# Feed-forward norms: VectorE adds the squares of tiles 1 to 3 only, TensorE sums the rest

## The chip, the cores and the metric

The kernel runs on one core of a Trainium2 chip. The metric is the device time of one execution in microseconds (us), as the median of several runs.

## The reference, cut to what matters

Two transformer blocks run one after the other on 256 tokens of 1024 channels in fp32. The first has neighbourhood attention and a routed mixture of experts and ends with a norm. The second has four layers; in each, attention of one of three kinds and a feed-forward part follow each other, each behind a norm:

```
def rms_norm_2(x, gain):
    var = jnp.mean(xf * xf, axis=-1, keepdims=True)
    return (xf * lax.rsqrt(var + EPS)).astype(x.dtype) * gain
...
    for i in range(DEPTH_2):
        h = modulate(rms_norm_2(x, norm_gain[i, 0]), sh1, sc1)
        ...
        x = x + g1 * y
        h = modulate(rms_norm_2(x, norm_gain[i, 1]), sh2, sc2)
        x = x + g2 * swiglu(h, ffn_w_gate[i], ffn_w_up[i], ffn_w_down[i])
```

The change touches the sum of squares of the second norm of each layer, the one in front of `swiglu`.

## The kernel before, in words

The residual stream `xT` stands transposed: 8 tiles (`KT`) of 128 channels by 256 tokens. A norm needs, for each token, the sum of squares over all 8 tiles and their 128 partitions. ScalarE squares tile by tile into `xsq` (line 1237, semaphore `sq_ready`). VectorE adds tiles 1 to 6 onto tile 0 of `xsq` (`add_squares`, line 1706, semaphore `sq_added`). TensorE multiplies a matrix of ones with tile 0 (line 525) and with tile 7 (line 527), which sums over partitions and leaves the result in every partition of a bank (`norm_of_sums`, semaphore `ssq_done`). ScalarE then takes a logarithm (1241) and an exponential (1243) into `rinv`; VectorE scales `xT` (1669), ScalarE adds the shift and rounds (1250), and VectorE makes the low part in `hT` (1680). Norms are numbered by `e`: 5, 7, 9 and 11 are the feed-forward norms of layers 0 to 3, and 6, 8 and 10 the first norms of layers 1 to 3.

All large products are made of three matmuls on a high and a low part (`split_product`, line 559). ScalarE casts a weight tile to its high part (1221, in `split`), and VectorE subtracts to get the low part (1962 for the output projection, 2179 for the first two gate tiles, 2199 and 2201 for the later ones). Each engine runs its own program in order; only semaphores tie them.

Around a feed-forward norm the orders are these. TensorE: the 8 tiles of the output projection, for layers 0 to 2 the first third of the next layer's modulation products (`group_rows`, 32 matmuls of line 617), `norm_of_sums`, for layers 0 to 2 the other two thirds (64 of line 617), and then the first two gate tiles, which take `hT` tile by tile. VectorE: for each output tile `update` (1696, adds the projection to `xT`); behind tile 5 `first_low(0)` and the adds of squares 1 to 3; behind tile 6 `first_low(1)` and the adds of squares 4 to 6; then `take_mods` (three small steps, 1806 to 1813), the update of tile 7, the split of gate tile 2 (2201), and the scaling. ScalarE: the squares of tiles 0 to 5, a cast, the squares of 6 and 7, the cast of gate tile 2, and then the logarithm. GpSimd's queue loads the modulation weights and waits for the matmuls of line 617 to free a buffer; SyncE's queue loads all other weights into a ring of three slots.

Of the kernel before, what the change touches and what calls it, by code (L numbers as in the profile page):

```python
# [14 lines left out]
KT = D // P  # L15
T = 256
# [63 lines left out]
def build(nc, ins, out):  # L80
# [3 lines left out]
    with ctx:  # L84
        offset = {}

        def sb(name, shape):
            offset[name] = -(-nc.sbuf_base // 32) * 32
            return ctx.enter_context(nc.sbuf_tensor(name, shape, F32))
# [5 lines left out]
        def sem(name):  # L95
            return ctx.enter_context(nc.semaphore(name))
# [7 lines left out]
        xsq = sb("xsq", [P, KT, T])  # L104
# [29 lines left out]
        def cst(name, lo=0, n=None):  # L134
            a, b = CONST[name]
            return const[:, a + lo:(a + lo + n) if n else b]

        def vc(name, lo=0, n=None):
            a, b = VEC[name]
            return vec[:, a + lo:(a + lo + n) if n else b]  # L140
# [21 lines left out]
        def split_views(ring, xsq, xn, hT, mixT, work, qk, qn, qr, vv):  # L162
# [56 lines left out]
        sq_added = sem("sq_added")  # L219
# [8 lines left out]
        sq_ready, ssq_done, ln_ms, rinv_ready, xn_ready, h_ready = (  # L228
            sem(n) for n in ("sq_ready", "ssq_done", "ln_ms", "rinv_ready", "xn_ready", "h_ready"))
# [115 lines left out]
        def group_of(i, part):  # L345

            return (0, 0, 1, 3)[part] if i == 0 else 4 * i + part
# [27 lines left out]
        def tiles_before(e):  # L375

            return KT * (e - (e > 3))

        def norm_bank(e):

            return bank[4 if e == 2 or e > 4 and e % 2 else 3]
# [128 lines left out]
        def _(pe):  # L510
            mm = nc.tensor.matmul
# [9 lines left out]
            def norm_of_sums(e):  # L521

                b = norm_bank(e)
                pe.wait_ge(sq_added, (KT - 2) * (e - 4))
                mm(b[:, 0:T], cst("ones"), xsq[:, 0, :], start=True, stop=False)
                pe.wait_ge(sq_ready, tiles_before(e) + KT)
                mm(b[:, 0:T], cst("ones"), xsq[:, KT - 1, :], start=False, stop=True).then_inc(ssq_done, 1)

            def norm_twice():

# [55 lines left out]
            def mix_out(d, k0, k1):  # L586

                n = FIRST["out_0"] + d // 4
                if d % 4 == 0 and k0 == 0:
                    wait_chunk(pe, n)  # L590
                b, at = MIX_TILES[d]
                for k in MIX_ORDER[k0:k1]:
                    m = mm(bank[b][:, at:at + T], chunk3(n, 512)[:, k, d % 4 * P:(d % 4 + 1) * P], mixT[:, k, :],  # L593
                           start=k == MIX_ORDER[0] and at == 0, stop=k == MIX_ORDER[-1], skip_group_check=True)
                return m
# [29 lines left out]
            def ada_columns(dst, row, c):  # L625

                out4 = dst.rearrange("p (h f c) -> p f h c", h=2, f=2)
                for f in range(2):
                    m = mm(out4[:, f], row[:, f * P:(f + 1) * P], cst("sel").rearrange("p (h c) -> p h c", h=2)[:, :, 0:c], start=True, stop=True)
                return m  # L630
# [17 lines left out]
            for n in range(N_HEAD):  # L648
                pe.wait_ge(rows_ready, n + 1)
                m = ada_columns(bank[2][:, 8 * n:8 * n + 8], ada_rows[:, n, :], 2)  # L650
            m.then_inc(ada_cols, 1)

            n = FIRST["mix"]
# [18 lines left out]
            for c in range(2):  # L672
                for t in range(TT):
                    m = mm(bank[4 + c][:, :], f3[:, t, c * P:(c + 1) * P], cst("dft", t * 2 * T, 2 * T), start=t == 0, stop=t == TT - 1)
            m.then_inc(dft_pe, 1)
            pe.wait_ge(dft_act, 2)
            for c in range(2):
                mm(bank[6 + c][:, 0:T], cst("cd"), soft[:, c, 0:T], start=True, stop=False)
                m = mm(bank[6 + c][:, 0:T], cst("sd"), soft[:, c, T:2 * T], start=False, stop=True)
# [3 lines left out]
            for f in range(2):  # L683
                for k in range(2):
                    m = mm(bank[4 + f][:, 0:T], wf[:, k, f * P:(f + 1) * P], prob[:, k, 0:T], start=k == 0, stop=k == 1)
# [68 lines left out]
            for d in range(6):  # L754
                m = mix_out(d, KT - 1, KT)
# [8 lines left out]
            for k in range(KT):  # L764
                pe.wait_ge(h_ready, KT * 2 + k + 1)
                for t in range(TT):
                    m = mm(bank[0][:, t * (G + E):(t + 1) * (G + E)], hT[:, k, t * P:(t + 1) * P], wr[:, k, :],
                           start=(k, t) == (0, 0), stop=k == KT - 1, skip_group_check=True)
            m.then_inc(route_done, 1)

            for t in range(TT):
                for k in range(KT):
                    m = nc.tensor.transpose(bank[4 + 2 * t + k // 4][:, k % 4 * P:(k % 4 + 1) * P], hT[:, k, t * P:(t + 1) * P], cst("ident"))
# [7 lines left out]
               start=False, stop=False, skip_group_check=True)  # L781
# [118 lines left out]
            def rest():  # L900
# [3 lines left out]
                for i in layers:  # L904
# [4 lines left out]
                    if i > 0:  # L909
                        norm_of_sums(4 + 2 * i)  # L910
                        group_rows(group_of(i, 2), "attn", 1)
# [737 lines left out]
        def _(dve):  # L1649
# [39 lines left out]
            def update(c, f, n, a, g):  # L1689

                if f < 3:
                    dve.wait_ge(y_done, MIX_DONE + 6 * (a - 1) + 3 * c + f + 1)
                else:
                    wait_used(dve, n)
                d = 4 * c + f
                V.scalar_tensor_tensor(xT[:, d, :], bank[(4 + d) % 8][:, 0:T], mod[:, g * KT + d:g * KT + d + 1], xT[:, d, :],
                                       ALU.mult, ALU.add).then_inc(x_done, 1)


            def add_squares(e, k0, k1):  # L1700

                for k in range(k0, k1):
                    dve.wait_ge(sq_ready, tiles_before(e) + k + 1)
                    if k > 1:
                        dve.wait_ge(sq_added, (KT - 2) * (e - 5) + k - 1)
                    V.tensor_tensor(xsq[:, 0, :], xsq[:, 0, :], xsq[:, k, :], ALU.add).then_inc(sq_added, 1)

            def normalise_in(e, src):
# [23 lines left out]
            n = FIRST["mix"] + 1  # L1732
# [68 lines left out]
            def take_mods(g):  # L1801

                chunks = chunks_of(g)
                i, lo, n = chunks[0] // 12, 4 * (chunks[0] % 12), 4 * len(chunks)
                dve.wait_ge(halves_landed, 64 * (g + 1))
                V.tensor_tensor(mod[:, lo:lo + n], halves[:, 0, 0:n], halves[:, 1, 0:n], ALU.add).then_inc(halves_sum, 1)
                dve.wait_ge(halves_sum, g + 1)
                V.tensor_tensor(mod[:, lo:lo + n], mod[:, lo:lo + n], vc("b_ada2", MODS * i + lo, n), ALU.add).then_inc(mods_taken, 1)
                dve.wait_ge(mods_taken, g + 1)
                if g == 0 or chunks[0] % 6 == 3:  # L1810
                    half = (chunks[-1] - 3) // 6 % 2
                    at = 3 * KT * half + KT
                    V.scalar_tensor_tensor(gain[:, 2 * half, :], mod[:, at:at + KT], 1.0, vc("gains2", (2 * i + half) * KT, KT),
                                           ALU.add, ALU.mult).then_inc(mods_ready, 1)
# [131 lines left out]
            for k in range(KT):  # L1946
                m = V.scalar_tensor_tensor(xT[:, k, :], xT[:, k, :], vc("normf", k, 1), rinv[:, :], ALU.mult, ALU.mult)
            then(m, "mods")

            for i in layers:  # L1950
# [7 lines left out]
                def low_out(c, f):  # L1958

                    n = FIRST[f"out_{i + 1}"] + c  # L1960
                    dve.wait_ge(attn_hi, out_splits(i) + 4 * c + f + 1)
                    V.tensor_tensor(part["w_gu"](n, f), full["w_gu"](n, f), w_out_hi[f][:, :, :].bitcast(F32),
                                    ALU.subtract).then_inc(attn_lo, 1)
# [211 lines left out]
                def first_low(f):  # L2175

                    dve.wait_ge(w_hi, 4 * split_count(i, 0) + f + 1)
                    n = FIRST[f"gu_{i}"]
                    V.tensor_tensor(part["w_gu"](n, f), full["w_gu"](n, f), w_out_hi[f].bitcast(F32), ALU.subtract).then_inc(w_lo, 1)

                for c in range(2):
                    for f in range(4):
                        if (c, f) == (1, 3):
                            take_mods(group_of(i, 3))
                        update(c, f, FIRST[f"out_{i + 1}"] + c, 1 + i, 2)
                        if c == 0:
                            low_out(1, f)
                        if (c, f) == (1, 1):
                            first_low(0)
                            add_squares(5 + 2 * i, 1, 4)  # L2190
                        if (c, f) == (1, 2):
                            first_low(1)
                            add_squares(5 + 2 * i, 4, KT - 1)
                def split(step, r, f, down=False):

                    dve.wait_ge(w_hi, 4 * split_count(i, step, down) + f + 1 + 4 * RING * r)
                    n = FIRST[f"down_{i}" if down else f"gu_{i}"] + step
                    if down:
                        m = V.tensor_tensor(part["w_down"](n, f), full["w_down"](n, f), part["whd"][f].bitcast(F32), ALU.subtract)  # L2199
                    else:  # L2200
                        m = V.tensor_tensor(part["w_gu"](n, f), full["w_gu"](n, f), part["whi"][f].bitcast(F32), ALU.subtract)  # L2201
                    m.then_inc(w_lo, 1)
# [199 lines left out]
```

## Time and profile before

| what | value |
|---|---|
| median of 3 runs | 2072.74 us (2072.51 to 2072.77) |
| the profiled execution's own time | 2074.49 us |
| its span from the first to the last instruction | 2072.7 us |
| mean granted TensorE clock | 0.974 |
| TensorE busy | 1886.8 us, 91% of the span |
| VectorE busy | 866.9 us, 42% |
| ScalarE busy | 721.5 us, 35% |
| adds of squares on VectorE (line 1706) | 42, 425 ns each |
| records of ones-matmuls (lines 525 and 527) | 14 and 14, two for each matmul |

Times are counted from the span's start. The four feed-forward norms lie at about 851, 1217, 1532 and 1868 us. A matmul's record is longer than the distance to the next one, because matmuls overlap; the chain of waits shows the distances.

### The profile page before, as it was taken

The numbers are of one execution on the slowest core, as the hardware profiler recorded it, in microseconds if no ns is written. First come the engines' busy times: TensorE is split into PE (matmuls) and PEld (weight loads), VectorE is DVE, ScalarE is ACT, GpSimd is POOL, SyncE is SP. The second block draws the span as 40 slices with busy tenths as digits, with TensorE's granted clock in tenths as the row PEclk, the third lists the DMA queues.
The fourth block names the chain that finished last, engine by engine and source line by source line (L and its number), as shares of the span: only waits on it lengthen the run. The fifth ranks groups of instructions, "written<-read, shape, count | busy, mean of one in ns | idle before, by whom it ended". The sixth has DMA issues, their size and how long they took to land.

```text
span 2072.7 us, 39160 instructions
## 1 busy us (share of the span) xinstructions
PE 1886.8 (91%) x16878; PEld 1605.2 (77%) x16878; DVE 866.9 (42%) x1512; ACT 721.5 (35%) x1237; POOL 72.8 (4%) x131
## 2 busy tenths in 40 slices
PE   6999976776677799999999999999999999999998
PEld 4788643444344588999987799998689998989998
DVE  0233311101010454654544565454864556555454
ACT  2111200000000355543432354353553444654443
POOL 0200000000000000100000010000010000000000
PEclk8999999899998999999999999999999999999999
DMA  9457899999999966753762485476284467324433
GB/s 397 190 223 297 328 426 427 428 427 428 427 428 427 422 241 240 300 199 140 287 267 99 164 324 186 155 290 274 93 339 180 177 267 311 130 112 163 172 144 133
DMA packets 42480, 552.48 MB, mean 267 GB/s; under 512 B 6528, under 2 KB 6912, under 8 KB 7040
## 3 DMA queue, kind: packets, MB, share of 16 engines
q1 hardware_dynamic: 33696, 454.17, 55.3%
q0 software_dynamic: 8672, 96.67, 11.3%
q8 instruction: 87, 1.43, 0.3%
q14 instruction: 25, 0.20, 0.0%
HBM read 549.58 MB, written 1.05 MB: 266 GB/s over the span
## 4 chain that ended last, share of the span: by engine, by line
PE 72%; DMA 21%; DVE 4%; ACT 2%; issue 1%; SPq 0%; DVEq 0%; ACTq 0%
PE bank L559 48%; DMA ada_ring<-in_moe_side 15%; PE bank L544 5%; PE bank L617 4%; DMA ring<-in_moe 3%; PE bank L553 2%; PE bank L824 2%; PE bank L593 1%; DMA ring<-in_v 1%; DMA ada_ring<-in_ada_last 1%; PE bank L1067 1%; PE bank L965 1%; PE bank L978 1%; ACT work L1478 1%; PE bank L602 1%
## 5 line engine op out<-in xcount | busy, mean ns | idle before, releaser
L559 PE MATMUL bank<-xsq_parts,ring_parts 128*128 128x256 f32 x1664 | 471.2, 283 | 0.0
L559 PEld LDWEIGHTS bank<-xsq_parts,ring_parts 128*128 128x128 f32 x1664 | 319.5, 192 | 0.0
L559 PE MATMUL bank<-xsq_parts,mixT_parts 128*128 128x256 f32 x704 | 199.2, 283 | 0.0
L559 PE MATMUL bank<-hT_parts,mixT_parts 128*128 128x256 f32 x704 | 199.2, 283 | 0.0
L1221 ACT CAST mixT_parts<-ring 128x1024 fp32r<-128x1024 f32 (+1 forms) x152 | 147.6, 999 | 112.5 <-PE bank L559 100.4
L559 PE MATMUL bank<-xsq_parts,xn_parts 128*128 128x256 f32 x640 | 181.1, 283 | 0.0
L559 PE MATMUL bank<-hT_parts,xn_parts 128*128 128x256 f32 x640 | 181.1, 283 | 0.0
L1895 DVE TENSOR_TENSOR mixT<-mixT,bank 128x128 f32<-128x128 f32 x32 | 9.2, 287 | 339.1 <-ACT mixT L1362 339.1
L559 PEld LDWEIGHTS bank<-xsq_parts,mixT_parts 128*128 128x128 f32 x704 | 135.2, 192 | 0.0
L559 PEld LDWEIGHTS bank<-hT_parts,mixT_parts 128*128 128x128 f32 x704 | 135.2, 192 | 0.0
L1221 ACT CAST xn_parts<-ring 128x1024 fp32r<-128x1024 f32 x96 | 100.0, 1050 | 96.3 <-PE bank L559 94.8
L559 PE MATMUL bank<-work_parts,mixT_parts 128*128 128x256 f32 x448 | 127.0, 284 | 0.0
L2201 DVE TENSOR_TENSOR ring_parts<-ring,xn_parts 128x1024 fp32r<-128x1024 f32 x80 | 97.7, 1225 | 68.4 <-ACT xn_parts L1221 65.7
L559 PEld LDWEIGHTS bank<-xsq_parts,xn_parts 128*128 128x128 f32 x640 | 122.9, 192 | 0.0
L559 PEld LDWEIGHTS bank<-hT_parts,xn_parts 128*128 128x128 f32 x640 | 122.9, 192 | 0.0
L824 PE MATMUL bank<-ada_ring,xsq 128*32 128x256 f32 x1024 | 76.8, 451 | 46.5 <-DMA ada_ring<-in_moe_side 46.5
L544 PE MATMUL bank<-hT,ring 128*128 128x256 f32 x512 | 116.1, 383 | 2.4 <-DMA ring<-in_na 1.7
L2199 DVE TENSOR_TENSOR ring_parts<-ring,mixT_parts 128x896 fp32r<-128x896 f32 x64 | 69.5, 1091 | 99.9 <-ACT mixT_parts L1221 99.9
L544 PEld LDWEIGHTS bank<-hT,ring 128*128 128x128 f32 x512 | 95.7, 190 | 19.2 <-issue 3.0
L2201 DVE TENSOR_TENSOR ring_parts<-ring,mixT_parts 128x1024 fp32r<-128x1024 f32 x88 | 104.2, 1222 | 13.7 <-ACT mixT_parts L1221 10.9
L824 PE MATMUL bank<-ring,xsq 128*32 128x256 f32 x1024 | 64.7, 396 | 44.3 <-DMA ring<-in_moe 43.5
L824 PEld LDWEIGHTS bank<-ada_ring,xsq 128*32 128x32 f32 x1024 | 34.5, 125 | 86.6 <-DMA ada_ring<-in_moe_side 62.5
(356 smaller groups left out, 4048.4 us busy)
## 6 DMA issues: line engine op xcount, KB each, us to landing
ring<-in_moe SPq DMA_DIRECT2D x48, 2048.0 KB, 27.2
ada_ring<-in_moe_side SPq DMA_DIRECT2D x48, 2048.0 KB, 26.0
ada_ring<-in_ada POOLq DMA_DIRECT2D x45, 2048.0 KB, 13.1
ring<-in_gu SPq DMA_DIRECT2D x44, 2048.0 KB, 7.7
ring<-in_down SPq DMA_DIRECT2D x32, 1408.0 KB, 6.3
ring<-in_na SPq DMA_DIRECT2D x12, 2048.0 KB, 10.3
ring<-in_out SPq DMA_DIRECT2D x10, 2048.0 KB, 8.2
ring<-in_qk SPq DMA_DIRECT2D x8, 2048.0 KB, 9.5
```

The costliest lines, as they stand in the source:

```text
L544: m = mm(dst, w[:, k, lo:lo + P], h[:, k, :], start=k == 0, stop=k == KT - 1)
L553: m = mm(dst[:, t, :], h[:, k, t * P:(t + 1) * P], w[:, k, lo:lo + n], start=k == 0, stop=k == KT - 1)
L559: m = mm(dst, w[a], x[b], start=start and (a, b) == (0, 0), stop=stop and a == 1, skip_group_check=shared)
L593: m = mm(bank[b][:, at:at + T], chunk3(n, 512)[:, k, d % 4 * P:(d % 4 + 1) * P], mixT[:, k, :], start=k == MIX_ORDER[0] and at == 0, stop= ...
L602: m = mm(o[64 * h:64 * h + 64, a:b], vv[:, kt, 64 * h:64 * h + 64], probT[:, h, c:d], start=i == 0, stop=i == len(tiles) - 1, skip_group_c ...
L617: m = mm(dst[32 * q:32 * q + 32, :], c[:, kk, :], w[:, kk, q % 2 * T:(q % 2 + 1) * T], start=k == 0, stop=k == 3)
L824: m = mm(bank[0][CAP * q:CAP * (q + 1), 0:T], xg[:, 4 * c + k, h * CAP:(h + 1) * CAP], w[:, k, q * T:(q + 1) * T], start=(c, k) == (0, 0), ...
L965: mm(bank[6 + h][:, 0:T], cst("suffix"), sp_[:, 0:T], start=True, stop=False, skip_group_check=True)
L978: m = mm(bank[4 + h][:, a:b], qk[hp, keys], qk[hp, tokens], start=True, stop=True)
L1221: return nc.scalar.copy(o, i)
L2199: m = V.tensor_tensor(part["w_down"](n, f), full["w_down"](n, f), part["whd"][f].bitcast(F32), ALU.subtract)
L2201: m = V.tensor_tensor(part["w_gu"](n, f), full["w_gu"](n, f), part["whi"][f].bitcast(F32), ALU.subtract)
```

## The change

For the feed-forward norms VectorE adds squares 1 to 3 only; the call for squares 4 to 6 is gone. TensorE multiplies ones with the summed tile 0 and then with tiles 4, 5, 6 and 7, one after the other, with a wait for each square. The layers' first norms keep six adds and two matmuls. As norms now differ in their number of adds, a helper counts the adds before a norm, and waits on `sq_added` use it.

```diff
@@
+        def adds_before(e):
+
+            return sum(3 if n % 2 else KT - 2 for n in range(5, e))
+
@@
             def norm_of_sums(e):
 
                 b = norm_bank(e)
-                pe.wait_ge(sq_added, (KT - 2) * (e - 4))
+                pe.wait_ge(sq_added, adds_before(e + 1))
                 mm(b[:, 0:T], cst("ones"), xsq[:, 0, :], start=True, stop=False)
-                pe.wait_ge(sq_ready, tiles_before(e) + KT)
-                mm(b[:, 0:T], cst("ones"), xsq[:, KT - 1, :], start=False, stop=True).then_inc(ssq_done, 1)
+                for k in range(1 + adds_before(e + 1) - adds_before(e), KT):
+                    pe.wait_ge(sq_ready, tiles_before(e) + k + 1)
+                    m = mm(b[:, 0:T], cst("ones"), xsq[:, k, :], start=False, stop=k == KT - 1)
+                m.then_inc(ssq_done, 1)
@@
                     if k > 1:
-                        dve.wait_ge(sq_added, (KT - 2) * (e - 5) + k - 1)
+                        dve.wait_ge(sq_added, adds_before(e) + k - 1)
@@
                         if (c, f) == (1, 2):
                             first_low(1)
-                            add_squares(5 + 2 * i, 4, KT - 1)
```

## Rows read from the trace of the kernel before

**Rows 1.** The page: shares of the chain that ended last, by engine.

```profile
PE 72%; DMA 21%; DVE 4%; ACT 2%; issue 1%; SPq 0%; DVEq 0%; ACTq 0%
```

**Rows 2.** Chain of waits, layer 0's norm: start us, us, what.

```profile
849.33 1.86 PE bank L617 x32
851.20 0.63 PE bank L525 x2
851.83 0.43 PE bank L527 x2
852.26 3.59 PE bank L617 x64
855.85 14.27 PE bank L559 x118
```

**Rows 3.** Timeline of VectorE, layer 0: start us, us, instruction [idle before].

```profile
853.25 1.28 DVE L1669 SCALAR_TENSOR_TENSOR xn<-xT,gain,rinv 128x256 f32<-128x256 f32 x3 [0.18 <-ACT rinv L1243]
854.44 0.48 DVE L1680 SCALAR_TENSOR_TENSOR hT_parts<-xn,mod,xsq_parts 128x256 fp32r<-128x256 f32 x1
```

**Rows 4.** Timeline of ScalarE, layer 0.

```profile
850.47 0.42 ACT L1237 ACTIVATE xsq<-xT 128x256 f32<-128x256 f32 x1 [3.00 <-DVE xT L1696]
...
852.29 0.48 ACT L1241 ACTIVATE xn<-bank,const_sb 128x256 f32<-128x256 f32 x1 [0.48 <-PE bank L527]
```

**Rows 5.** Timeline of TensorE, layer 0.

```profile
851.66 0.59 PE L527 MATMUL bank<-xsq,const_sb 128*128 128x256 f32 x2
...
855.78 0.38 PE L559 MATMUL bank<-xsq_parts,w_out_hi 128*128 128x256 f32 x1
```

**Rows 6.** Waits: TensorE from 1871 us on; the load queue, 852 to 1870.

```profile
PE bank L559 <- DVE hT_parts L1680: 3.2, 1, 3.2
...
SPq L436 <- PE bank L559: 779.9, 69, 28.4
```

**Rows 7.** Timeline of TensorE, layer 3.

```profile
1865.96 0.28 PE L559 MATMUL bank<-mix_hi,ring_parts 128*128 128x256 f32 x1
1866.52 0.70 PE L525 MATMUL bank<-xsq,const_sb 128*128 128x256 f32 x2 [0.27 <-DVE xsq L1706]
1867.84 0.70 PE L527 MATMUL bank<-xsq,const_sb 128*128 128x256 f32 x2 [0.63 <-ACT xsq L1237]
1871.71 0.55 PE L559 MATMUL bank<-xsq_parts,w_out_hi 128*128 128x256 f32 x1 [3.17 <-DVE hT_parts L1680]
```

**Rows 8.** Timeline of VectorE, layer 3.

```profile
1864.98 1.48 DVE L1706 TENSOR_TENSOR xsq<-xsq 128x256 f32<-128x256 f32 x3
...
1866.86 0.48 DVE L1696 SCALAR_TENSOR_TENSOR xT<-bank,mod,xT 128x256 f32<-128x256 f32 x1
1868.76 1.23 DVE L2201 TENSOR_TENSOR ring_parts<-ring,mixT_parts 128x1024 fp32r<-128x1024 f32 x1 [1.42 <-ACT mixT_parts L1221]
1869.90 1.27 DVE L1669 SCALAR_TENSOR_TENSOR xn<-xT,gain,rinv 128x256 f32<-128x256 f32 x3
```

**Rows 9.** Timeline of ScalarE, layer 3.

```profile
1867.37 0.42 ACT L1237 ACTIVATE xsq<-xT 128x256 f32<-128x256 f32 x1 [2.99 <-DVE xT L1696]
1867.70 1.03 ACT L1221 CAST mixT_parts<-ring 128x1024 fp32r<-128x1024 f32 x1
1868.63 0.46 ACT L1241 ACTIVATE xn<-bank,const_sb 128x256 f32<-128x256 f32 x1
```

**Rows 10.** Windows, layer 3: us, busy PE, PEld, DVE, ACT, POOL, PEclk, DMA share, GB/s.

```profile
1866.00:1869.00 3.00, 1.64 (x7) 0.64 (x5) 1.48 (x6) 1.63 (x3) 0.00 (x0) 1.00 0.57 126
1869.00:1871.70 2.70, 0.00 (x0) 0.02 (x1) 2.70 (x6) 1.74 (x5) 0.00 (x0) 0.57 1.01 431
1871.70:1876.10 4.40, 4.39 (x20) 4.40 (x21) 4.40 (x12) 3.05 (x7) 0.00 (x0) 0.50 0.31 130
```

**Rows 11.** Windows, layer 2's attention.

```profile
1492.00:1494.50 2.50, 0.89 (x4) 0.52 (x6) 2.40 (x8) 2.11 (x9) 0.00 (x0) 1.00 0.92 393
1494.50:1498.00 3.50, 3.15 (x38) 2.23 (x39) 3.36 (x13) 1.17 (x5) 0.00 (x0) 1.00 0.53 227
```

## The prediction

> **What bounds the kernel now.** I read four views, in this order. The page first: the chain that ended last lies 72% on TensorE, 21% on transfers and 4% on VectorE [rows 1]. So VectorE's time as such is worth nothing; the question is whether VectorE stands in front of TensorE at the four places that change. Second, the chain of waits around the feed-forward norm of layer 0 [rows 2]. The reader is to see that it stays on TensorE without a break: 1.86 us for 32 matmuls of the next layer's modulation (L617), 0.63 us for the ones-matmul over the summed tile (L525), 0.43 us for the one over tile 7 (L527), 3.59 us for 64 more of L617, then the first gate and up tiles (L559). Layers 1 and 2 repeat it row for row. Third, the timelines of the three engines there [rows 3 to 5]. The last square is ready at 850.47 + 0.42 = 850.89 us; TensorE takes it up at 851.66, so it came 0.77 us early. The logarithm starts at 852.29, 0.04 us after the record of L527 ends (851.66 + 0.59 = 852.25). The first split tile hT is there at 854.44 + 0.48 = 854.92 us, and TensorE comes to it at 855.78, 0.86 us later. Fourth, the waits [rows 6]: TensorE's longest wait in layer 3's feed-forward stretch is 3.2 us, behind the norm, and of the four changed places this is the only one behind which it stands still. The load queue's waits are on TensorE alone, 779.9 us in the largest row, so no transfer sets a pace that could swallow a delay of TensorE.
>
> **Layers 0 to 2.** The change takes tiles 4 to 6 out of the sum on VectorE (three adds, 1.48 us for the three) and gives TensorE three more ones-matmuls between L525 and L527. VectorE's saving is worth nothing here: it brings the update of tile 7, its square and the cast behind it forward, and the square was already 0.77 us early. Squares 4 to 6 are older than that, so the three new matmuls wait for nothing. They are three more of what the row of L527 shows, a ones-matmul that follows another one: 0.43 us each [rows 2]. The bound above is the 0.63 us of L525, which has a change of operands in front of it; the bound below is 0, if the matmuls could slip under other work, and the unbroken chain excludes that. I take 0.43, because the weights stay the same and the neighbours are of one kind, as for L527. That is 3 x 0.43 = 1.29 us for a layer. Does a cover swallow it? The 0.86 us with which hT is early can't: logarithm, exponential and scaling hang on the last ones-matmul, so hT moves back by the same 1.29 us as the 64 matmuls of L617 in front of the gate tiles. TensorE is behind on both sides equally. Queued behind the new matmuls are L617, for whose buffers GpSimd's load queue waits (it needs them for the next group, far ahead), and the logarithm on ScalarE. Nothing else is queued that could be late first. Three layers: 3 x 1.29 = +3.87 us.
>
> **Layer 3.** There is no next layer, so no L617 fills the gap and VectorE does stand in front. L525 waits for VectorE's last add and starts at 1866.52 us, though TensorE's last output-projection matmul ends at 1865.96 + 0.28 = 1866.24 [rows 7]. On VectorE the three adds begin at 1864.98 and the update of tile 7 at 1866.86; without them the small modulation steps between (1866.86 - 1864.98 - 1.48 = 0.40 us) are over by 1865.4, before 1866.24, and by the 0.04 us seen above the update can start at 1866.28, 0.58 us earlier [rows 8]. So can the square (1867.37 to 1866.79), the cast of gate tile 2 (1867.70 to 1867.12) and the split of it on VectorE (1868.76 to 1868.18) [rows 8, 9]. Square 7 is then ready at about 1867.2. TensorE, from 1866.24, needs 0.63 + 4 x 0.43 = 2.35 us for the five ones-matmuls and ends at 1868.59, against 1867.84 + 0.70 = 1868.54 before. TensorE is now the last for the sum and the logarithm stays at 1868.63. But scaling on VectorE started only at 1869.90, held by the split. In layer 0 it started 853.25 - 852.29 = 0.96 us after the logarithm [rows 3, 4], which gives 1868.63 + 0.96 = 1869.59 here, and the split is over by then. So 0.31 us are won. Bounds: 0, if the split still holds it, and 0.58, the whole shift. Sum: +3.87 - 0.31 = +3.56 us.
>
> **The clock.** The chip lowers TensorE's granted clock to 0.50 while it stands still behind this norm (0.57 as a mean over 1869.0 to 1871.7), and the first 4.40 us of gate tiles run at 0.50, 20 matmuls begun [rows 10]. At full clock a matmul of the kind takes 14.27 / 118 = 0.121 us [rows 2], so 20 would take 2.42 us: the low clock costs 1.98 us. Before the change TensorE is busy for 1.64 of the 3 us from 1866 to 1869; the change closes its two gaps there and shortens the idle stretch behind from 3.17 us to about 2.8 (1868.59 to 1871.40). That can only help the clock, by 0 to 1.98 us, but the stretch stays long. I take 0.2 us, the tenth part of what it costs, and the sum is +3.36 us, +3.4 rounded. The Trainium skill ("TensorE: Matmul & The Clock Gate", section "What's actually happening") says that the chip's measuring of activity isn't tied to a kernel's start, so that the moment of a change varies between runs. No row here shows it; if it holds, what this term gives in one execution need not be what the timed ones give.
>
> **Sum.** The profiled execution took 2074.49 us around a span of 2072.7; the median of the runs is 2072.74, 1.75 less. The change is a difference inside the span, so I add it to the median: 2072.74 + 3.4 = 2076.1 us, 0.16% more. About 0.2%, 4.15 us, is what a measurement of this kernel can tell from no change.
>
> **Rivals.**
> - The clock takes instead of giving: slower. The added 1.29 us of each layer move all later work against the moments at which the clock changes. In layer 2's attention TensorE has 0.89 us of work in the 2.5 us from 1492 to 1494.5 and still keeps the full clock [rows 11]. If it falls there, the 3.15 us of work in the next 3.5 us take up to 3.15 us longer, about half of it on the chain: +1.6 us. In layer 3 a low stretch that lies wholly on busy TensorE instead of partly on its idle time (from 1869.4 or so to 1871.7) costs up to 1.2 us more. It decides from 0.8 us of added loss, where +3.4 passes +4.15. Either gives about +5.0: 2077.8. For it: such thinly used stretches exist. Against: the clock is full at this one, and the changed one is as likely to come to a better moment. 12%.
> - The clock gives all of the 1.98 us back: 3.56 - 1.98 = +1.6, so 2074.3. For it: TensorE is now busy up to 1868.59. Against: 2.8 us of idleness remain. The same page (section "HAM oscillation — how this bites in real kernels") says that idle gaps between bursts bring the low clock back each time; by it this term stays at a loss near 1.98, and the trace agrees at this one place (0.50 behind the gap). 10%.
> - The matmuls cost more than 0.43 us, for example because each looks at a semaphore of its own: halfway to 0.63, 0.53 us, makes 9 x 0.53 - 0.31 - 0.2 = +4.3, so 2077.0, and 0.63 would make +5.2, 2077.9. Against: L527 has such a look and costs 0.43. 5%.
> - VectorE was what held every norm, and freeing it wins 0.58 us four times: 2072.74 - 2.3 = 2070.4. It needs TensorE to wait for the last square by more than the 1.29 us added. Against: the square is 0.77 us early. 3%.
>
> **How the numbers follow.** The forecast has 70%. Its own spread is about 1 us, so it holds a little of both the cases above: slower by over 0.2% gets 12 + 5 + 3 = 20%, within 0.2% 79%, faster 1%, for the last rival together with a returned clock. The range has to take in the returned clock and a little below it (2073.5) and the clock's loss (2078.0).
>
> **What would show it.** The profile of the changed kernel should have 30 adds of squares instead of 42, and 52 records of ones-matmuls instead of 28 (two records for each matmul, 12 more matmuls). In layers 0 to 2 the chain should show 1.7 us where it has 0.43 behind L525, no wait of TensorE there, the first gate tile 1.3, 2.6 and 3.9 us later than before, and hT still early by about 0.86. In layer 3 L525 follows the projection without a gap, scaling starts 0.3 us sooner against it, and the clock still falls. Wrong it would be if TensorE waited in front of L527 in layers 0 to 2, if the new matmuls took 0.6 us each, or if a low clock turned up between 852 and 1866 us.

## The result and the profile after

The changed kernel takes 2077.35 us against 2072.62 us for the kernel before, medians of 20 runs each. The ratio is 1.002, with a 95% interval of 1.0014 to 1.0026, or 2.9 to 5.4 us. The forecast was 2076.1 us (+3.4) in a range of 2073.5 to 2078.0. The time lies in the range, 1.2 us above the forecast. The medians are 4.7 us apart, more than the 4.15 us (0.2%) that the prediction took as the least that can be told from no change, and the interval reaches from below that mark to above it: "within 0.2%" and "slower" cannot be told apart here.

The profiled execution took 2076.92 us, with a span of 2074.2. The page has 1500 instructions on VectorE instead of 1512 and 24 more matmul records, which are 12 matmuls. By line there are 30 adds of squares and 14 + 38 = 52 records of ones-matmuls:

```profile
L1712 DVE TENSOR_TENSOR xsq<-xsq x30: 417/425/426, 843.2 to 1865.5; 128x256 f32<-128x256 f32 x30
```

```profile
L532 PE MATMUL bank<-xsq,const_sb x38: 378/379/379, 849.7 to 1870.4; 128*128 128x256 f32 x38
```

The lines have moved: L525 and L527 are now L529 (the summed tile) and L532 (tiles 4 to 7), L617 is L623, L559 is L565, L1669 is L1675, L1706 is L1712, L2201 is L2206. The chain of waits at layer 0's norm, to be held against [rows 2]:

```profile
847.41 1.86 PE bank L623 x32
849.27 0.63 PE bank L529 x2
849.90 1.73 PE bank L532 x8
851.63 3.59 PE bank L623 x64
855.22 14.87 PE bank L565 x123
```

Each row is what it was, and 0.43 us has become 1.73: 1.30 us for three matmuls. (All of it starts 1.9 us earlier than before, because the part of the program ahead of it ended earlier in this execution.) TensorE still does not wait. The timeline of VectorE there:

```profile
847.45 0.48 DVE L1702 SCALAR_TENSOR_TENSOR xT<-bank,mod,xT 128x256 f32<-128x256 f32 x1 [0.73 <-PE bank L565]
849.35 1.23 DVE L2206 TENSOR_TENSOR ring_parts<-ring,mixT_parts 128x1024 fp32r<-128x1024 f32 x1 [1.42 <-ACT mixT_parts L1227]
852.62 1.28 DVE L1675 SCALAR_TENSOR_TENSOR xn<-xT,gain,rinv 128x256 f32<-128x256 f32 x3 [2.05 <-ACT rinv L1249]
853.81 0.48 DVE L1686 SCALAR_TENSOR_TENSOR hT_parts<-xn,mod,xsq_parts 128x256 fp32r<-128x256 f32 x1
```

The time that VectorE got back has turned into waits: 0.73 us for the projection before the update of tile 7, and 2.05 us for `rinv` where [rows 3] has 0.18. The first tile of `hT` is there at 853.81 + 0.48 = 854.29 us, and TensorE's first gate matmul starts at 855.15: early by 0.86 us, as before.

Layer 3, the chain:

```profile
1854.90 13.76 PE bank L565 x115
1868.66 0.02 issue
1868.68 0.49 DVE xT L1702
1869.18 0.02 issue
1869.20 0.42 ACT xsq L1243
1869.62 0.94 ACT mixT_parts L1227
1870.56 0.02 issue
1870.58 1.23 DVE ring_parts L2206
1871.81 1.27 DVE xn L1675 x3
1873.07 0.41 DVE hT_parts L1686
1873.48 0.14 issue
1873.62 128.41 PE bank L565 x1056
```

The update of tile 7 now follows the projection's last matmul at once; in [rows 7, 8] 0.62 us lay between (1866.24 to 1866.86). From the end of the projection to the first gate tile it is 1873.62 - 1868.65 = 4.97 us instead of 1871.71 - 1866.24 = 5.47. TensorE there:

```profile
1868.48 0.59 PE L529 MATMUL bank<-xsq,const_sb 128*128 128x256 f32 x2
1868.91 1.89 PE L532 MATMUL bank<-xsq,const_sb 128*128 128x256 f32 x8
1873.62 0.35 PE L565 MATMUL bank<-xsq_parts,w_out_hi 128*128 128x256 f32 x1 [2.81 <-DVE hT_parts L1686]
```

The five ones-matmuls follow without a gap, 0.43 us each from the first (1868.48 to 1868.91), and the wait behind them is 2.81 us instead of 3.17. The windows, for the clock (layer 2's attention, then the idle stretch and the first gate tiles of layer 3):

```profile
1492.00:1494.50 2.50, 0.71 (x3) 0.30 (x2) 2.40 (x8) 2.11 (x8) 0.00 (x0) 1.00 0.87 354
1494.50:1498.00 3.50, 3.23 (x19) 2.36 (x19) 2.96 (x11) 1.23 (x6) 0.00 (x0) 0.61 0.64 274
...
1871.00:1873.60 2.60, 0.00 (x0) 0.01 (x1) 2.60 (x6) 1.95 (x5) 0.00 (x0) 1.00 0.89 365
1873.60:1878.00 4.40, 4.38 (x24) 4.40 (x25) 4.40 (x12) 3.05 (x7) 0.00 (x0) 0.61 0.44 190
```

In layer 2's attention the clock reads 0.61 where [rows 11] has 1.00; behind layer 3's norm it falls only when the gate tiles have begun, and reads 0.61 over them where [rows 10] has 0.50.

**A ruler.** What lies ahead of layer 0's norm varied by 4.5 us between the profiles of all kernels of the study (stretch A below began at 846.01 to 850.50 us). So I compare stretches of the chain: A from the 32 modulation matmuls in front of layer 0's norm to those of layer 1's, B on to layer 2's, C on to the end of layer 3's projection, D on to the first gate tile, and R, the rest, to the end of TensorE's last matmul. The clock can fall in three places of it: in layer 2's attention (in B), over the first gate tiles behind layer 3's norm, and in layer 3's last down product from about 2006 us on (both in R).

| kernel | A | B | C | D | R | all |
|---|---|---|---|---|---|---|
| before | 365.70 | 314.84 | 336.37 | 5.47 | 195.60 | 1217.98 |
| changed | 366.86 | 316.68 | 337.70 | 4.97 | 195.11 | 1221.32 |

The difference of the profiles is +1.16, +1.84, +1.33, -0.50 and -0.49: +3.34 us, where +3.36 had been forecast.

### The profile page after: what moved, and what is told of

Same layout as the page of the kernel before. It is cut to its first block, busy times and chain, and to the rows that moved or that the text cites. A ratio compares the mean times of both kernels' runs of the same rounds, so it can differ in the third digit from the quotient of the medians.

```text
span 2074.2 us, 39184 instructions
## 1 busy us (share of the span) xinstructions
PE 1892.2 (91%) x16902; PEld 1609.5 (78%) x16902; DVE 863.0 (42%) x1500; ACT 721.8 (35%) x1237; POOL 72.8 (4%) x131
## 4 chain that ended last, share of the span: by engine, by line
PE 72%; DMA 20%; DVE 4%; ACT 2%; issue 1%; SPq 0%; POOL 0%; DVEq 0%; ACTq 0%
PE bank L565 48%; DMA ada_ring<-in_moe_side 19%; PE bank L550 5%; PE bank L623 5%; PE bank L830 2%; PE bank L559 2%; PE bank L599 1%; PE bank L1073 1%; PE bank L971 1%; DMA ring<-in_ada_head 1%; PE bank L984 1%; ACT work L1484 1%; PE bank L608 1%; PE bank L962 1%; PE bank L522 1%
## 5 line engine op out<-in xcount | busy, mean ns | idle before, releaser
L565 PE MATMUL bank<-xsq_parts,ring_parts 128*128 128x256 f32 x1664 | 471.0, 283 | 0.0
L565 PEld LDWEIGHTS bank<-xsq_parts,ring_parts 128*128 128x128 f32 x1664 | 319.3, 192 | 0.0
L565 PE MATMUL bank<-xsq_parts,mixT_parts 128*128 128x256 f32 x704 | 199.2, 283 | 0.0
L565 PE MATMUL bank<-hT_parts,mixT_parts 128*128 128x256 f32 x704 | 199.2, 283 | 0.0
L565 PE MATMUL bank<-xsq_parts,xn_parts 128*128 128x256 f32 x640 | 181.1, 283 | 0.0
L565 PE MATMUL bank<-hT_parts,xn_parts 128*128 128x256 f32 x640 | 181.1, 283 | 0.0
L565 PEld LDWEIGHTS bank<-xsq_parts,mixT_parts 128*128 128x128 f32 x704 | 135.2, 192 | 0.0
L565 PEld LDWEIGHTS bank<-hT_parts,mixT_parts 128*128 128x128 f32 x704 | 135.2, 192 | 0.0
L565 PE MATMUL bank<-work_parts,mixT_parts 128*128 128x256 f32 x448 | 127.0, 284 | 0.0
L2206 DVE TENSOR_TENSOR ring_parts<-ring,xn_parts 128x1024 fp32r<-128x1024 f32 x80 | 97.7, 1225 | 67.8 <-ACT xn_parts L1227 65.2
L565 PEld LDWEIGHTS bank<-xsq_parts,xn_parts 128*128 128x128 f32 x640 | 122.9, 192 | 0.0
L565 PEld LDWEIGHTS bank<-hT_parts,xn_parts 128*128 128x128 f32 x640 | 122.9, 192 | 0.0
L2206 DVE TENSOR_TENSOR ring_parts<-ring,mixT_parts 128x1024 fp32r<-128x1024 f32 x88 | 104.2, 1223 | 13.8 <-ACT mixT_parts L1227 11.0
```

The source lines that it names most:

```text
L565: m = mm(dst, w[a], x[b], start=start and (a, b) == (0, 0), stop=stop and a == 1, skip_group_check=shared)
```

## The experiments

Common to all: "outside" is the time of an execution less its span. Each median of the kernel before is of runs timed together with the experiment's.

**Layer 3 alone.** Three adds and five matmuls in the last norm, six adds and two matmuls in layers 0 to 2.

```diff
-            return sum(3 if n % 2 else KT - 2 for n in range(5, e))
+            return sum(3 if n == 3 + 2 * LAYERS else KT - 2 for n in range(5, e))
...
                             first_low(1)
+                            if i + 1 in layers:
+                                add_squares(5 + 2 * i, 4, KT - 1)
```

> The change in layer 3's norm alone; layers 0 to 2 as before. I look at the median and at the stretch of the chain from the first modulation matmuls in front of layer 0's norm to the end of TensorE's last matmul (before: 849.33 to 2067.32, 1217.99 us; changed kernel: 847.41 to 2068.73, 1221.32 us), which leaves out what varies ahead of it. Theory (TensorE is the bound in layers 0 to 2, VectorE in layer 3): the stretch is 0.3 to 0.6 us shorter than before, up to 1 us more or less by the clock, the median 0 to 1 us below before. Rival (the three matmuls cost wherever they stand): the stretch 1 to 1.3 us longer.

Measured: 2071.93 us (12 runs) against 2073.11 (31 runs), ratio 0.9992 (0.9983 to 1.0). Chain: A 365.53, B 315.76, C 336.37, D 4.97, R 195.11, all 1217.74. So the part in layer 3 wins its 0.5 us by itself, and A and C are back to what they were. B is 0.92 longer although its work is the same; its windows show the clock at 0.50 in layer 2's attention:

```profile
1489.00:1492.00 3.00, 0.95 (x4) 0.31 (x3) 2.86 (x10) 2.62 (x10) 0.00 (x0) 0.98 0.83 344
1492.00:1495.00 3.00, 2.98 (x16) 2.03 (x16) 2.33 (x9) 0.90 (x4) 0.00 (x0) 0.50 0.63 270
```

That is what the first rival priced at up to 1.6 us: 0.9 here, 0.5 in the changed kernel's profile. The medians lie 1.2 us apart where 0 to 1 was expected; the interval, 0 to 3.5 us, holds both.

**VectorE's saving alone.** The adds of squares 4 to 6 are gone everywhere, no matmul takes their place.

```diff
-                for k in range(1 + adds_before(e + 1) - adds_before(e), KT):
+                for k in range(KT - 1, KT):
```

> VectorE's adds of squares 4 to 6 are gone in all four feed-forward norms and no matmul is added: the sums leave out tiles 4, 5 and 6, so part of the norm is not computed. This is VectorE's saving alone. Theory: nothing in layers 0 to 2, 0.58 us in layer 3: stretch 1217.4, median about 0.6 us below before. Rival (VectorE holds every norm): 4 x 0.58, stretch 1215.7, median 2.3 us below before.

Measured: 2071.30 us (12 runs) against 2073.11, ratio 0.9991 (0.9983 to 1.0). Chain: A 365.57, B 315.75, C 336.38, D 4.89, R 194.40, all 1216.99. Twelve adds fewer win 0.58 us, in layer 3, and nothing in layers 0 to 2 (A is 0.13 shorter, as it is by 0.17 in the kernel above, which has all its adds there). The rival in which VectorE holds every norm is out. The rest of the difference is the clock's: B is 0.91 longer, as above, and R 1.20 shorter, 0.5 of it over the gate tiles and 0.7 behind them, where before the clock also fell in the last down product and here it did not (a window of the kernel before, then one of this kernel, whose down product starts 2.5 us earlier):

```profile
2006.60:2008.60 2.00, 2.00 (x12) 2.00 (x11) 2.00 (x4) 2.00 (x5) 0.00 (x0) 0.50 0.00 0
```

```profile
2004.00:2006.00 2.00, 1.43 (x13) 1.26 (x12) 2.00 (x5) 2.00 (x5) 0.00 (x0) 1.00 0.00 0
```

The 1.8 us between the medians are therefore no measure of the adds.

**TensorE's cost alone.** All adds stay; three ones-matmuls come in front, their sums overwritten.

```diff
                 b = norm_bank(e)
+                if e % 2:
+                    for k in range(4, KT - 1):
+                        pe.wait_ge(sq_ready, tiles_before(e) + k + 1)
+                        mm(b[:, 0:T], cst("ones"), xsq[:, k, :], start=True, stop=True)
                 pe.wait_ge(sq_added, (KT - 2) * (e - 4))
```

> VectorE adds all six squares as before; in the feed-forward norms TensorE does three more ones-matmuls, on tiles 4 to 6, ahead of its two, and their sums are overwritten. This is TensorE's cost alone. Theory: 9 x 0.43 = 3.9 us in layers 0 to 2, nothing in layer 3, where they lie in TensorE's waits: stretch 1221.9, median 3.9 above before. Rival (a matmul with a wait of its own costs 0.53 to 0.63): 4.8 to 5.7.

Measured: 2077.12 us (12 runs) against 2073.11, ratio 1.002 (1.0012 to 1.0029). Chain: A 366.85, B 316.11, C 337.67, D 5.47, R 193.90, all 1220.00. The cost is there without any saving, +1.15 to +1.30 us a layer, and the price is 0.43 us. In layer 3 it is nothing. The median is 4.0 us above before, as expected (3.9), but not for the expected reason: on the chain it is only 2.02 us, and another 1.0 us, of which more below, lies outside the span. R is 1.70 shorter than before, because the clock did not fall behind layer 3's norm:

```profile
1874.40:1879.00 4.60, 4.56 (x35) 4.51 (x36) 4.60 (x12) 3.25 (x7) 0.00 (x0) 1.00 0.29 125
```

That gives what the low clock of [rows 10] cost: 1.7 us, not the 1.98 that I had put in. TensorE stands still for 3.17 us in front of these gate tiles, exactly as long as before, where the clock fell.

**Twice the dose.** No adds in the feed-forward norms, eight matmuls.

```diff
-            return sum(3 if n % 2 else KT - 2 for n in range(5, e))
+            return sum(0 if n % 2 else KT - 2 for n in range(5, e))
...
-                pe.wait_ge(sq_added, adds_before(e + 1))
+                pe.wait_ge(sq_added, adds_before(e + 1)) if e % 2 == 0 else pe.wait_ge(sq_ready, tiles_before(e) + 1)
...
                             first_low(0)
-                            add_squares(5 + 2 * i, 1, 4)
```

> VectorE adds no squares in the feed-forward norms, TensorE takes all eight tiles: six more matmuls than before, twice the dose. Theory: 3 x 6 x 0.43 = 7.7 us in layers 0 to 2; in layer 3 TensorE needs 0.63 + 7 x 0.43 = 3.64 us from 1866.24, so the logarithm comes at 1869.92 and the scaling at 1870.88, 1.0 later than before. Sum +8.7: stretch 1226.7, median 2081.3. Rival (0.53 a matmul): +10.8. If the difference of the changed kernel beyond 3.4 us is no price of a matmul but chance or the clock, this one keeps to +8.7 and does not show twice the excess.

Measured: 2079.93 us (7 runs) against 2073.11, ratio 1.003 (1.0019 to 1.0041). Chain: A 368.14, B 317.42, C 338.94, D 6.26, R 194.89, all 1225.65. Against the kernel with the change in layer 3 alone, A has 2.61 us more for six matmuls, C 2.57: 0.43 each. In layer 3 TensorE is now the bound; the chain of the norm is all its own:

```profile
1871.52 0.43 PE bank L529 x2
1871.95 3.04 PE bank L532 x14
1874.99 0.02 issue
1875.01 0.48 ACT xn L1247
```

The whole is 1.0 us under the forecast, of which D makes 0.19, A to C 0.15, and the rest is in R, where the clock fell later than before. The medians differ by 6.8 us (3.9 to 8.5), so the 8.7 that was forecast is missed and the chain's 7.7 is not. Twice the excess does not show.

**The opposite direction.** In layers 0 to 2 VectorE adds all seven squares and TensorE has one matmul; for that the update of tile 7 goes ahead of the modulation steps. Layer 3 as changed.

```diff
-            return sum(3 if n % 2 else KT - 2 for n in range(5, e))
+            return sum(KT - 2 if n % 2 == 0 else 3 if n == 3 + 2 * LAYERS else KT - 1 for n in range(5, e))
...
-                mm(b[:, 0:T], cst("ones"), xsq[:, 0, :], start=True, stop=False)
+                m = mm(b[:, 0:T], cst("ones"), xsq[:, 0, :], start=True, stop=adds_before(e + 1) - adds_before(e) == KT - 1)
...
-                        if (c, f) == (1, 3):
+                        if (c, f) == (1, 3) and i + 1 not in layers:
                             take_mods(group_of(i, 3))
                         update(c, f, FIRST[f"out_{i + 1}"] + c, 1 + i, 2)
+                        if (c, f) == (1, 3) and i + 1 in layers:
+                            take_mods(group_of(i, 3))
+                            add_squares(5 + 2 * i, KT - 1, KT)
...
                             first_low(1)
+                            if i + 1 in layers:
+                                add_squares(5 + 2 * i, 4, KT - 1)
```

> The opposite direction in layers 0 to 2: VectorE adds all seven squares (the update of tile 7 goes ahead of the modulation steps, then the add of square 7), and TensorE has one ones-matmul instead of two; layer 3 as changed (three adds, five matmuls). Theory (each ones-matmul of layers 0 to 2 costs TensorE 0.43 us, and VectorE's time there is free): the sum is ready at about 850.9 us, before TensorE comes to it at 851.1, so 0.43 us are won in each of three layers, 1.3, and 0.5 in layer 3: stretch 1216.2 (plus up to 1 us for the clock), median 1.8 us below before. Rival (the added square comes late and TensorE waits for it): nothing or a loss of up to 0.5 us in each layer, stretch 1217.5 to 1219.

Measured: 2069.74 us (9 runs) against 2073.75 (17 runs), ratio 0.9981 (0.9971 to 0.9991): 4.0 us faster, with an interval from 1.9 to 6.0 us, whose near end is the 1.8 that was expected. Chain: A 365.15, B 314.94, C 335.97, D 4.97, all 1215.89, 2.1 less than before:

```profile
849.25 1.86 PE bank L623 x32
851.11 0.63 PE bank L529 x2
851.74 3.59 PE bank L623 x64
855.33 14.75 PE bank L565 x122
```

The 0.43 us of the second matmul is gone, and nothing waits. Of all kernels of the study it has the shortest stretch and the lowest median. The chain accounts for 2.1 of the 4.0 us; the other 1.9 no row explains, and the interval does not tell them from nothing.

**The changed kernel again,** with nothing edited.

> The changed kernel once more, for the size of the difference (3.4 us forecast, 4.7 between the medians) and for another draw of the clock. Theory: the steps of the chain come out the same to 0.1 us (1.3 us more in each of layers 0 to 2, 0.5 less in layer 3 up to the first gate tile) wherever the clock is full, and the stretch differs from 1221.3 only by where the clock falls, within 1 us either way. The ratio stays between 1.0014 and 1.0026. Rival (the excess over 3.4 us is a cost of the change in some other place): a stretch of 1222.5 or more.

Measured: 2078.90 us (9 runs) against 2073.75, ratio 1.0025 (1.0015 to 1.0035). Chain: A 366.86, B 316.15, C 337.66, D 4.97, R 193.93, all 1219.57. The steps come out as in the first profile but for the clock, which now stays full both in layer 2's attention (B is 0.53 shorter) and over layer 3's first gate tiles (R is 1.18 shorter):

```profile
1872.00:1874.70 2.70, 0.00 (x0) 0.00 (x1) 2.70 (x6) 2.06 (x5) 0.00 (x0) 1.00 0.96 388
1874.70:1879.00 4.30, 4.27 (x33) 4.22 (x34) 4.30 (x12) 2.95 (x7) 0.00 (x0) 1.00 0.41 175
```

The ratio, 1.0025, lies where it was expected, and the stretch is well under the rival's 1222.5. But the stretch is only 1.6 us over before, and yet the median difference is 5.15. Part of this is which executions were profiled: that of before took 1.9 us more than its kernel's median, 2072.62, and this one 1.9 less than its own. The rest has to be missing from the ruler. Outside the span, the changed kernel's runs have 2.72 to 2.93 us (20 runs) and here 2.70 to 3.00 (9), the kernel before 1.73 to 1.83 in all of its 31 and 17 runs. The kernel with only the matmuls added has 2.73 to 2.95; the other four have 1.74 to 1.87. That is 1.0 us which no row of the span holds. The last five runs look for it; each is one execution.

**Two matmuls more a norm** (VectorE adds 1 to 4).

```diff
-            return sum(3 if n % 2 else KT - 2 for n in range(5, e))
+            return sum(4 if n % 2 else KT - 2 for n in range(5, e))
...
                             first_low(1)
+                            add_squares(5 + 2 * i, 4, 5)
```

> VectorE adds squares 1 to 4 in the feed-forward norms, TensorE takes 0, 5, 6 and 7: two matmuls more a norm than before, 8 in all. For the chain: 2 x 0.43 us in each of layers 0 to 2 (+2.6), 0.5 less in layer 3: stretch 1217.98 + 2.1 = 1220.1, up to 1 us more or less by the clock. For the time outside the span (execution time less span), which was 1.75 to 1.87 us in every run of before and of the kernels with 0, 3 and 24 matmuls more, and 2.70 to 3.00 in every run of the three with 12 more: theory (it hangs on what the program looks like as loaded, not on work done): 1.8 or 2.8, nothing in between. Rival (it grows with TensorE's added work): 8 matmuls give about 2.4.

Measured: A 366.42, B 315.68, C 337.26, D 4.90, all 1219.89. Outside 1.8 us.

**Four more a norm** (VectorE adds 1 and 2).

```diff
-            return sum(3 if n % 2 else KT - 2 for n in range(5, e))
+            return sum(2 if n % 2 else KT - 2 for n in range(5, e))
...
-                            add_squares(5 + 2 * i, 1, 4)
+                            add_squares(5 + 2 * i, 1, 3)
```

> VectorE adds squares 1 and 2 only: four matmuls more a norm than before, 16 in all. Chain: 3 x 4 x 0.43 = +5.2 in layers 0 to 2, 0 in layer 3 (six matmuls there end 0.43 later than the changed kernel's five, which takes its 0.5 back): stretch 1223.1. Outside the span: theory 1.8 or 2.8; rival 3.1.

Measured: A 367.26, B 317.08, C 338.09, D 5.40, all 1222.92. Outside 1.9 us.

**The changed kernel with twelve overwritten matmuls in layer 3.**

```diff
+                if e == 3 + 2 * LAYERS:
+                    pe.wait_ge(sq_ready, tiles_before(e) + 6)
+                    for k in range(12):
+                        mm(b[:, 0:T], cst("ones"), xsq[:, 4 + k % 2, :], start=True, stop=True)
                 pe.wait_ge(sq_added, adds_before(e + 1))
```

> The changed kernel with 12 more ones-matmuls, whose sums are overwritten, in front of layer 3's norm: 24 more than before in all, as many as the kernel in which TensorE takes all eight tiles. Chain: 12 x 0.43 = 5.2 us more than the changed kernel, all in layer 3: stretch 1226.5. Outside the span: if the number of TensorE's matmuls in the program decides, 1.8 us as in that kernel, the changed kernel's extra 1.0 us gone although more is done; if something else that the changed kernel has decides, 2.8 stays.

Measured: D 10.15, 5.18 more than the changed kernel, 0.43 a matmul; all 1225.93. Of the 0.6 us to the expected 1226.5, 0.53 is layer 2's attention, where the clock stays full here (B 316.15) and fell in the profile from which I had counted. Outside 1.9 us: with more work the extra 1.0 us is gone.

**One fewer and two more,** both in layer 3 only: a fourth add instead of a matmul, and two overwritten matmuls.

```diff
-            return sum(3 if n % 2 else KT - 2 for n in range(5, e))
+            return sum(4 if n == 3 + 2 * LAYERS else 3 if n % 2 else KT - 2 for n in range(5, e))
...
+                            if i + 1 not in layers:
+                                add_squares(5 + 2 * i, 4, 5)
```

> The changed kernel with a fourth add and one matmul fewer in layer 3 only: 11 matmuls more than before. Chain: as the changed kernel in layers 0 to 2; in layer 3 the sum ends 0.43 us sooner, but the split of gate tile 2 still holds VectorE, so only 0.08 is won: 4.9 from the end of the projection to the first gate tile. Outside the span, if the number of TensorE's matmuls in the program decides: either 1.8 (12 lies at an edge) or 2.8 (a band around 12).

```diff
+                if e == 3 + 2 * LAYERS:
+                    pe.wait_ge(sq_ready, tiles_before(e) + 6)
+                    for k in range(2):
+                        mm(b[:, 0:T], cst("ones"), xsq[:, 4 + k, :], start=True, stop=True)
                 pe.wait_ge(sq_added, adds_before(e + 1))
```

> The changed kernel with two more ones-matmuls in layer 3, whose sums are overwritten: 14 more than before. Chain: 0.86 us more than the changed kernel, in layer 3: 5.8 from the end of the projection to the first gate tile. Outside the span: 1.8 or 2.8, as in the run with 11; together they show how wide the band is in which the extra 1.0 us stands (16 gave 1.9).

Measured: D 4.90 and 5.84. Outside 2.0 us with 11 more matmuls and 1.8 with 14. The 2.0 is a single reading; it lies above the 1.73 to 1.87 of all other kernels without the extra, and far below 2.70.

| matmuls more than before | 0 | 3 | 8 | 11 | 12 | 14 | 16 | 24 |
|---|---|---|---|---|---|---|---|---|
| outside, us | 1.8 | 1.8 | 1.8 | 2.0 | 2.8 | 1.8 | 1.9 | 1.8 to 1.9 |
| runs | 71 | 12 | 1 | 1 | 41 | 1 | 1 | 8 |

## Why the forecast was right, and where it was off

**Layers 0 to 2: mechanism and size right.** TensorE was the bound, each of the nine added matmuls cost it 0.43 us, and VectorE's saving was worth nothing; the two runs that do one half of the change each show both halves. It shows best from the modulation matmuls in front of a feed-forward norm to those in front of the next layer's first norm, a stretch in which the clock is full in every profile. In layer 0 it starts at 849.33 us before and at 847.41 us changed, and it ends at the first and the second of these rows:

```profile
1051.04 1.86 PE bank L617 x32
```

```profile
1050.41 1.86 PE bank L623 x32
```

| ones-matmuls in the norm | kernels | layers 0, 1, 2: us |
|---|---|---|
| 1 | seven added | 201.28, 201.28, 201.28 |
| 2 | before; layer 3 alone | 201.71, 201.71, 201.71 |
| 2 | adds gone | 201.70, 201.70, 201.71 |
| 4 | two matmuls more | 202.56, 202.56, 202.57 |
| 5 | changed | 203.00, 203.01, 203.00 |
| 5 | matmuls only | 203.00, 203.00, 203.01 |
| 6 | four matmuls more | 203.43, 203.43, 203.43 |
| 8 | none added | 204.30, 204.29, 204.29 |

The change costs 1.29, 1.30 and 1.29 us there, 3.88 against 3.87 forecast. By the ruler it is less in the second profile of the changed kernel, 1.16 + 1.31 + 1.29 = 3.76, and the reason lies in the profile of before, in a place that the change does not touch. The first 21 matmuls of layer 1's output projection take 2.87 us there and 2.71 in the changed kernel, at a full clock in both, and the kernel with layer 3 alone changed has 2.71 too. What the 0.16 us are is open.

```profile
1189.70 2.87 PE bank L559 x21
```

```profile
1189.12 2.71 PE bank L565 x21
```

**The whole chain, 3.34 us against 3.36 forecast, agrees that well by luck.** It is 3.88, less 0.13 for layer 1 (A), plus 0.54 for the clock in layer 2's attention (B), plus 0.04 elsewhere in C, less 0.50 in layer 3 (D) and 0.49 behind it (R). The forecast had no term for the first three of these differences, and the other two it had at another size.

**Layer 3: sign right, the term mis-sized, and another engine last:** 0.50 us won, 0.31 forecast. The step was "TensorE, from 1866.24, needs 0.63 + 4 x 0.43". The 0.63 was read from a place where the ones-matmul follows the modulation's narrower matmuls. Behind the projection's full-width ones it costs 0.43 and starts before the projection's last record ends, so TensorE finished sooner and the logarithm did not hold the scaling. The split of gate tile 2 did: at 1871.81 VectorE goes from it to the scaling without a pause. With two or four matmuls and the shorter adds D is 4.89 and 4.90, with five 4.97, and from there on it grows by 0.43 each: 5.40 with six, 5.84 with seven, 6.26 with eight. So five matmuls are just about what fits.

**The clock: no one term of -0.2 us exists.** In the first profile it was two things, 0.49 us won behind layer 3's norm and about 0.53 lost in layer 2's attention, where the first rival had put it (at up to 1.6). The prediction had named a low clock between 852 and 1866 us as a sign that it would be wrong; the sign came (0.61 from 1494.5 to 1498), but it did not mean that: the second profile of the same kernel lacks it, and the kernel whose layers 0 to 2 are as before has it. In the second profile nothing was lost there and 1.7 won. The two profiles are of one and the same kernel, so the change does not decide where the clock falls. In 6 of the 13 profiles it falls in layer 2's attention and costs 0.5 to 0.9 us. Over the first gate tiles it stays full in three, behind idle stretches of 2.8 and 3.2 us, so such a gap does not bring the low clock back each time, as the rule beside the second rival has it; the rows decide against it. The Trainium skill ("TensorE: Matmul & The Clock Gate", section "What's actually happening") says that the chip's measuring of activity isn't tied to the kernel's start and that the effect is variable from run to run; the trace agrees, 0.61 against 1.00 over the same gate tiles.

**What the forecast had not: 1.0 us outside the span.** The step was "the change is a difference inside the span, so I add it to the median". It failed: 2.8 us outside instead of 1.8, in all 29 runs of the changed kernel that were timed. With the clock as it was before, the sum is 3.76 - 0.50 + 1.0 = +4.3 us, inside both intervals (2.9 to 5.4 and 3.1 to 7.3); the medians, +4.7 and +5.2, leave 0.5 to 0.9 us that these intervals cannot tell from nothing. That the time fell in the range is owed in part to the range, which was made wide for the clock and not for this. The 1.0 us is not work: 12 more matmuls have it and 14, 16 and 24 don't. It goes with the number of matmuls in TensorE's program in every kernel here: two with 12 that share little else have it (six adds with three overwritten matmuls; three adds with five), and the padded one does not. The number of all instructions does not decide: 39192 are in the page of the kernel with only the matmuls added (2.73 to 2.95) and in that of four matmuls more a norm (1.9). The counts 8, 11, 14 and 16 and the padded kernel rest on one execution each. What makes the 1.0 us is open, and so is whether other counts have it.

**The rivals.** VectorE as the holder of every norm fell: with its adds gone A and C stay within 0.13 us and only D is shorter. The dearer matmul fell: 0.43 at every dose. The clock taking and the clock giving both happened: the first profile has some of each, the second only the giving.

## What to carry to other kernels

In these kernels work moved from an idle engine to the one that the chain stays on cost its full price, down to a piece of 0.43 us. Before moving such work, look whether the busy engine waits at that place, and judge the places one by one. Here the same edit lost 1.3 us at three norms and won 0.5 at the fourth, and doing it in the one and its opposite in the three others gave a kernel 4 us faster than before (1.9 to 6.0), 2.1 us of it on the chain. When a difference is around 0.1%, compare the time outside the span too: a fixed microsecond can sit there.

## What the runs showed of the hardware that was not expected

- Time outside the span: 1.73 to 1.87 us in every run of before and of four other kernels, 2.70 to 3.00 in all 41 runs of the two kernels with exactly 12 more matmuls in TensorE's program; see the table above.
- A ones-matmul in fp32 on 256 columns leaves two records and costs 0.43 us in a row of its kind (1.73 us for 8 records, 0.216 each); behind the modulation matmuls, whose weights are 32 columns wide, the first costs 0.63, behind full-width ones of 128 columns 0.43. The Trainium skill ("TensorE: Matmul & The Clock Gate", section "Wait — 56ns, not 53.3ns?") gives 215.7 ns as the spacing of matmuls of 512 columns at full clock; the trace shows the same number for each of the two records of 256 columns.
- A low clock over the first gate tiles cost 1.7 us where all 4.40 us lay in it, and 1.2 where it fell 0.5 us after they began. It cost 2.4 in the kernel with two matmuls more a norm, where it lasted 6.1 us into them: the row of 1056 matmuls behind the norm is 129.62 us there, and 127.24 with the clock full. Behind one and the same wait of 3.17 us it was 0.50 in the kernel before and 1.00 in the kernel with only the matmuls added.
